# Statistics of x for the recurrent stage: made tile by tile in the experts' tail instead of at the stage's head

## The reference

```python
x = x + gate2[:, None, :] * grouped_moe(h, ...)      # end of the first block
...
def _rmsnorm(x, g):
    x32 = x.astype(jnp.float32)
    y = x32 * lax.rsqrt(jnp.mean(x32 * x32, axis=-1, keepdims=True) + EPS)
    return (y * g.astype(jnp.float32)).astype(x.dtype)

mem_n = _rmsnorm(mem, g_mem)
for _ in range(DEPTH):                               # DEPTH = 1
    h = _rmsnorm(x, g_mix)
    proj = h @ w_in
```

## Time and profile before

| | us |
|---|---|
| median of 3 runs | 2318.85 |
| lowest, highest | 2314.3, 2320.19 |
| the profiled execution | 2319.08 |
| its span | 2317.3 |
| PE, DVE, ACT, POOL busy | 2121.6, 1119.1, 864.4, 577.1 |

### The profile page before, as it was taken

One profiled execution on the slowest core, in us unless ns is written; L12 is line 12 of the kernel. 1 busy time (PEld: TensorE's weight loads), 2 busy tenths in 40 slices (PEclk: granted clock), 3 DMA queues, 4 the chain that ended last, 5 costly groups with the idle time before them and its releaser, 6 DMA issues. The chain is left out here.

```text
span 2317.3 us, 23519 instructions
## 1 busy us (share of the span) xinstructions
PE 2121.6 (92%) x9422; PEld 1601.8 (69%) x9422; DVE 1119.1 (48%) x1387; ACT 864.4 (37%) x1084; POOL 577.1 (25%) x195
## 2 busy tenths in 40 slices
PE   6997999999879999879999969899799998999997
PEld 3766755474358888767777747687388876887886
DVE  3344556646780234658888547405722245223223
ACT  4441223334222223457677437524423233221221
POOL 0421200130024344100000103430244343433431
PEclk9998999999989999889999989999799999999999
DMA  7223223231023233379999922231023232322210
GB/s 241 91 85 147 84 98 126 93 109 32 0 65 127 85 106 109 116 268 375 361 385 383 328 70 91 93 92 46 2 90 100 90 111 91 109 96 85 91 55 37
DMA packets 174702, 299.15 MB, mean 129 GB/s; under 512 B 8927, under 2 KB 66474, under 8 KB 174600
## 3 DMA queue, kind: packets, MB, share of 16 engines
q1 hardware_dynamic: 169256, 279.40, 35.4%
q0 software_dynamic: 3040, 9.93, 1.2%
q10 hardware_dynamic: 2304, 8.39, 0.9%
HBM read 274.57 MB, written 23.13 MB: 128 GB/s over the span
## 5 line engine op out<-in xcount | busy, mean ns | idle before, releaser
L130 POOL TENSOR_TENSOR region<-weights,region 128x2048 fp32r<-128x2048 f32 (+2 forms) x94 | 366.0, 3896 | 943.7 <-ACT region L124 764.5
L240 PE MATMUL ps<-region 128*128 128x512 f32 (+1 forms) x1336 | 530.8, 397 | 33.3 <-DVE region L130 10.9
L244 PE MATMUL ps<-region 128*128 128x512 f32 (+1 forms) x1336 | 520.6, 390 | 0.0
L243 PE MATMUL ps<-region 128*128 128x512 f32 (+1 forms) x1336 | 520.5, 390 | 0.0
L240 PEld LDWEIGHTS ps<-region 128*128 128x128 f32 x1336 | 259.6, 194 | 98.0 <-issue 19.4
L243 PEld LDWEIGHTS ps<-region 128*128 128x128 f32 x1336 | 259.5, 194 | 52.8 <-issue 4.1
L244 PEld LDWEIGHTS ps<-region 128*128 128x128 f32 x1336 | 259.2, 194 | 50.7
L124 ACT ACTIVATE region<-weights 128x2048 fp32r<-128x2048 f32 (+2 forms) x98 | 158.5, 1622 | 285.7 <-PE ps L244 236.8
L2870 DVE TENSOR_TENSOR region<-weights,region 128x2048 fp32r<-128x2048 f32 x92 | 209.4, 2289 | 71.2 <-ACT region L2794 71.1
L2794 ACT ACTIVATE region<-weights 128x2048 fp32r<-128x2048 f32 x92 | 176.2, 1917 | 89.4 <-PE ps L2711 30.8
L281 PE MATMUL ps<-region 128*128 128x512 f32 x480 | 190.1, 396 | 7.0 <-DVE region L3769 4.4
(11 more groups left out here) (417 smaller groups left out, 2773.0 us busy)
## 6 DMA issues: line engine op xcount, KB each, us to landing
weights<-w_in SPq DMA_DIRECT2D x54, 1024.0 KB, 5.2
weights<-moe_w_gate SPq DMA_DIRECT2D x32, 1024.0 KB, 7.6
weights<-moe_w_up SPq DMA_DIRECT2D x32, 1024.0 KB, 8.9
weights<-moe_w_down SPq DMA_DIRECT2D x32, 1024.0 KB, 7.0
weights<-w_mod SPq DMA_DIRECT2D x24, 1024.0 KB, 5.6
weights<-w_mlp_in SPq DMA_DIRECT2D x16, 1024.0 KB, 5.2
weights<-w_mlp_out SPq DMA_DIRECT2D x16, 1024.0 KB, 5.0
h_slots<-region SPq DMA_DIRECT2D x16, 512.0 KB
```

The source lines that it names most:

```text
L130: eng.tensor_tensor(flat(self.part(K, n, 1)), flat(self.ring.view(n)), flat(self.part(K, n, 0)).bitcast(F32), ALU.subtract).then_inc(self. ...
L240: ins = pe.matmul(out, l_hi, r_hi, start=(start and k == 0), stop=False)
L243: pe.matmul(out, l_hi, r_lo, start=False, stop=False)
L244: ins = pe.matmul(out, l_lo, r_hi, start=False, stop=(stop and k == kt - 1))
```

## The change

The sums are made for one tile of 128 tokens at a time in the tail of `moe_stage`. For each tile ACT squares all 1024 channels in one instruction (`square`), POOL folds the eight channel tiles to four and to two (two additions, 512 and 256 wide), PE sums the two over the channels with products by ones (`squares`), ACT takes the root (`root`) and DVE inverts it. PE turns tile 0 between `memory(1)` and `memory(2)`, DVE adds tile 0 to x before it combines tiles 2 and 3, and ACT takes its squares of tiles 0 and 1 before the copy of `memory(3)`, those of 2 and 3 behind it. In the overflow stage the statistics are made anew, with `NormStats`, after the loop and within the branch. `lru_stage` makes none: it scales two tiles at once and rounds its second weight chunk after four tiles of the norm.

```diff
@@ moe_stage @@
+    x_sq = (K.at(148, KD, P), K.at(164, KD, P))
+    def token_sums(t):
+        return K.ps[:, MEM_BANKS[t % 2], t * P:(t + 1) * P]
@@ POOL, behind the gathers @@
+            for t in range(ST):
+                sq = x_sq[t % 2]
+                pool.wait_ge(x_squared, t + 1)
+                pool.tensor_tensor(sq[:, 0:4, :], sq[:, 0:4, :], sq[:, 4:8, :], ALU.add).then_inc(x_folded, 1)
+                pool.wait_ge(x_folded, 2 * t + 1)
+                pool.tensor_tensor(sq[:, 0:2, :], sq[:, 0:2, :], sq[:, 2:4, :], ALU.add).then_inc(x_folded, 1)
@@ PE @@
-            memory(0, False)
-            memory(1, False)
-            arrived(K, pe, n_mem + 2)
-            memory(2, True)
-            for t in range(ST):
+            def turn_out(t):
                 pe.wait_ge(summed, t + 1)
                 if t >= 2:
                     pe.wait_ge(x_added, KD * (t - 1))
...
+            def squares(t):
+                pe.wait_ge(x_folded, 2 * t + 2)
+                if t >= 2:
+                    pe.wait_ge(x_rooted, t - 1)
+                for k in range(2):
+                    ins = pe.matmul(token_sums(t), K.ones[:, :], x_sq[t % 2][:, k, :], start=(k == 0), stop=(k == 1))
+                ins.then_inc(x_summed, 1)
+            memory(0, False)
+            memory(1, False)
+            turn_out(0)
+            arrived(K, pe, n_mem + 2)
+            memory(2, True)
+            turn_out(1)
+            turn_out(2)
+            turn_out(3)
             pe.wait_ge(y_out, 2 * NEXP)
             memory(3, False)
-            pe.wait_ge(mem_out, 1)
-            pe.matmul(K.ps[:, MEM_BANKS[0], 0:1], K.ones[:, :], K.ones[:, 0:1], start=True, stop=True).then_inc(r.used, 2)
+            pe.wait_ge(mem_out, 3)
+            pe.matmul(K.ps[:, MEM_BANKS[2], 0:1], K.ones[:, :], K.ones[:, 0:1], start=True, stop=True).then_inc(r.used, 2)
+            for t in range(ST):
+                squares(t)
@@ ACT @@
+            def square(t):
+                act.wait_ge(x_added, KD * (t + 1))
+                if t >= 2:
+                    act.wait_ge(x_summed, t - 1)
+                act.activation(x_sq[t % 2], K.xT[:, :, t * P:(t + 1) * P], ACT.Square).then_inc(x_squared, 1)
+            def root(t):
+                act.wait_ge(x_summed, t + 1)
+                act.activation(K.rstd[:, t * P:(t + 1) * P], token_sums(t), ACT.Sqrt, bias=K.eps, scale=1.0 / D)\
+                    .then_inc(x_rooted, 1)
             memory(2)
+            square(0)
+            square(1)
             memory(3)
+            root(0)
+            square(2)
+            root(1)
+            square(3)
+            root(2)
+            root(3)
@@ DVE @@
+            combine(0)
+            combine(1)
+            add_to_x(0)
+            combine(2)
+            combine(3)
+            for t in range(1, ST):
+                add_to_x(t)
+            for t in range(ST):
+                root = K.rstd[:, t * P:(t + 1) * P]
+                dve.wait_ge(x_rooted, t + 1)
+                dve.reciprocal(root, root).then_inc(x_inverted, 1)
+            dve.wait_ge(x_inverted, ST)
@@ moe_overflow_stage @@
+    stats = NormStats(K, stat_signals, K.xT, S, K.at(108, 2, S), K.rstd, 6)
...
         with eng.If(count > 0):
             with eng.Fori(0, count) as i:
                 body(i)
+            if again:
+                again(count)
@@ lru_stage, PE @@
-            for t in range(KD):
-                stats.add(pe, t)
@@ lru_stage, ACT @@
             split.high(K, act, n0)
-            for t in range(KD):
-                stats.square(act, t)
+            norm.act(act, 0, 4)
             split.high(K, act, n0 + 1)
-            stats.root(act)
-            norm.act(act)
+            norm.act(act, 4, KD)
@@ lru_stage, DVE @@
+            norm.scale(dve, 0)
+            norm.scale(dve, 1)
             split.low(K, dve, n0)
-            stats.invert(dve)
-            dve.wait_ge(stats.inverted, 1)
-            norm.dve(dve, 0, 4)
+            norm.rest(dve, 0)
+            norm.rest(dve, 1)
+            norm.dve(dve, 2, 4)
             split.low(K, dve, n0 + 1)
```

More of the change, by code:

```diff
@@ L24 @@
 NMARKS = 16
-NSIG = 24
+NSIG = 29
 VECS = [("c", 8), ("c_ctx", 8), ("b_mod", 48), ("norm1_g", 8), ("norm2_g", 8), ("q_norm_g", 1), ("k_norm_g", 1),
@@ L2644, in moe_stage @@
      y_out, even_y_stored, odd_y_stored, weighed, summed, x_turned, x_added, mem_done, mem_out, mem_rec, mem_root,
-     scaled) = K.signals(24)
+     scaled, x_squared, x_folded, x_summed, x_rooted,
+     x_inverted) = K.signals(29)
     rows_in, y_stored = (even_rows_in, odd_rows_in), (even_y_stored, odd_y_stored)
@@ L2911, in _, with combine @@
             low_hidden(NEXP - 1)
-            for t in range(ST):
+            def combine(t):
                 b = both[:, t, 0, :]
@@ L2916, in _, with add_to_x @@
                     .then_inc(summed, 1)
-            for t in range(ST):
+            def add_to_x(t):
                 dve.wait_ge(x_turned, t + 1)
@@ L2922, in _ @@
                                              mod_col(K, 5, c), x, ALU.mult, ALU.add).then_inc(x_added, 1)
-            dve.wait_ge(x_added, ST * KD)
+            combine(0)
[10 more added lines that the diff above has]
+            dve.wait_ge(x_inverted, ST)
 def moe_order():
@@ L2939, in moe_overflow_stage @@
     T = K.T
-    came, freed, gu_done, silu_done, up_done, hid_done, down_done, x_added = K.signals(8)
+    came, freed, gu_done, silu_done, up_done, hid_done, down_done, x_added, *stat_signals = K.signals(12)
     FT = 4
@@ L2945, in moe_overflow_stage, with experts @@
     LOADS = 7
+    stats = NormStats(K, stat_signals, K.xT, S, K.at(108, 2, S), K.rstd, 6)
     def part(s):
         return w[:, s, :].rearrange("p (t c) -> p t c", c=HALF)
-    def experts(eng, body):
+    def experts(eng, body, again=None):
         count = eng.value_load(K.over_list[0:1, NEXP:NEXP + 1], min_val=0, max_val=NEXP)
@@ L2989, in body, with again @@
                                 for k in range(FT)]).then_inc(down_done, 1)
-            experts(pe, body)
+            def again(count):
+                for t in range(KD):
+                    stats.add(pe, t)
+            experts(pe, body, again)
         @block.scalar
@@ L2998, in body, with again @@
                     act.activation(silu[:, f % 2, :], K.ps[:, f % 2, :], ACT.Silu).then_inc(silu_done, 1)
-            experts(act, body)
+            def again(count):
+                act.wait_ge(freed, count + 1)
+                for t in range(KD):
+                    stats.square(act, t)
+                stats.root(act)
+            experts(act, body, again)
         @block.vector
@@ L3023, in body, with again @@
                 dve.memset(prod[:, 0, 2:3], 0.0).then_inc(freed, 1)
-            experts(dve, body)
+            def again(count):
+                stats.invert(dve)
+                dve.wait_ge(stats.inverted, 1)
+            experts(dve, body, again)
 def lru_stage(K):
@@ L3034, in lru_stage @@
     n0, nq = r.first("lru"), r.first("qm")
-    stats = NormStats(K, norm_signals[0:4], K.xT, S, K.at(92, 4, S), K.rstd, 5)
-    norm = NormApply(K, norm_signals[4:7], K.xT, (K.h_hi, K.h_lo), gain_of(K, "g_mix_2"), None, K.rstd, K.at(100, KD, S))
+    norm = NormApply(K, norm_signals[0:3], K.xT, (K.h_hi, K.h_lo), gain_of(K, "g_mix_2"), None, K.rstd, K.at(100, KD, S))
     nX, nG = (n0, n0 + 2), (n0 + 4, n0 + 6)
```

## The result

The changed kernel takes 2304.84 us, the median of 6 runs (2298.67 to 2308.34); the kernel before 2316.75 (2313.39 to 2320.19, 6 runs). The ratio is 0.9945, 95% interval 0.993 to 0.996, a gain of 12.7 us (9.3 to 16.2).

What follows compares the result with a forecast made beforehand. TensorE, busy 92% of a 2317.3 us span, bounds the kernel, so changes pay where it stands still. Head -13.35 plus tail +5.5 gives -7.9 us, from 2319.08 to 2311.2, stated as 2311.0 for the median; range 2306 to 2316.

Steps and rivals of the forecast that it cites:

- Rival 1: Overflow stage: its instruction page was held up by weight transfers, some 1.5 us of queueing, so 2309.5 us; chance 0.17.
- The rule on fetches: Overflow stage: a taken branch to outside the two instruction pages held must wait for a fetch; no size given.
- The head: Start of the recurrent stage to its first product: 5.07 us instead of 18.42, saving 13.35.
- The tail: End of the experts' stage: the added statistics chain makes it end 5.5 us later.
- The order's 3.4 us: Experts' tail: with tile 0 turned and added earlier, the last product of the memory ends 3.4 us earlier.
- the chain behind the last product: Experts' tail: copy, table load, roots, squares, foldings, small products and reciprocal, from 1345.2 to 1355.7.
- Rivals 2 to 4: ACT stalls at table switch, 2312.4 us (0.07); slow clock lasts longer, 2313.5 (0.12); POOL foldings cost more, 2325.7 (0.06).

Runs made afterwards that it cites:

- e1: The kernel before with ten one-column TensorE products (40 instructions) added ahead of the overflow branch; ratio 0.9987.
- e3: The changed kernel with 24 one-column TensorE products (96 instructions) added inside the overflow branch that is not taken; ratio 0.9962.
- e4: The changed kernel with the product that frees two weight slots moved behind the four sums, so two transfers fall into the overflow stage; ratio 0.9961.
- e2: The kernel before with two weight chunks issued in the recurrent stage instead of at the end of the experts' tail; ratio 0.9989.
- e5: The changed kernel with the old order of the experts' tail: tile 0 turned after the third memory product, all tiles combined before additions; ratio 0.9952.
- e7: The changed kernel with all four squares and the table load ahead of ACT's copy of the last memory product; 2298.86 us, ratio 0.9909.

## Why the prediction was wrong

- **The step that failed** is "The overflow stage stays at 6.07 us (1350.16 to 1356.23): its new instructions stand inside the branch not taken." It fell to 2.22. The step took a body that is never run to cost nothing, and the jump over it at its old price. What counts is also how many TensorE instructions stand ahead of the branch and in it: in the profiles e1 makes the stage 3.85 us shorter with padding alone, and e3 makes it 3.17 longer again with padding that is never run. Each was done with one size of padding, so where the page's edges lie was not measured. The run times do not show this step by themselves (e1 has no gain inside its interval, e3 and e4 have the same ratio). Had I asked the view of the branch's line for its own duration, the 4.79 us would have been in the sum's bounds.
- **Rival 1** had the right place and the wrong cause and price. It gave 1.5 us to queueing behind the weights. Without transfers the jump still takes 3.71 us (e2) and 4.12 (e3) against 4.79, so queueing is 0.7 to 1.1 us and is not what went: with the weights back the stall stays away (e4). The prediction also had the landing early: the packet ran from 1353.34 to 1354.45 and so landed 4.3 us into the stage, not 3.4.
- **The rule on fetches** was cited with the row and then used for nothing but queueing. By the Trainium skill (Runtime: NRT & Kernel Launch, Instruction fetch mechanics) a taken branch stalls if its target lies outside the two pages held. The traces agree with it: the jump takes 0.46 to 0.48 us in the seven kernels in which no page's packet came during it, and 3.71 to 4.79 us in the three in which one did (before, e2, e3).
- **The head** was right: 4.98 us measured, 5.07 forecast, 13.44 saved against 13.35.
- **The tail** was right: +5.34 against +5.5. Its prices by what the trace has: table load 1.28 (1.28), root 0.37 (0.36), square 1.05 (1.05), foldings 1.27 and 0.72 (1.29 and 0.65), small products 1.22 (0.9; the granted clock stood at 0.50 there), reciprocal 0.95 (0.95). The order's 3.4 us is borne out by before and after (3.3 to 3.8) and by e5 (3.0 to 3.6, through a disturbed profile), and the chain behind the last product took 10.7 us against 10.5.
- **Rivals 2 to 4** fell. The gap between the load's end and the root is 0.01 us, and e7 recovers 1.22 us and not 2.7. The foldings took 2.0 us a pair, 4.0 for the four where 3.9 was priced. The low clock lasted shorter, not longer: in the 5.4 us behind the first product the mean clock is 0.70 and 17 records run, against 0.50 and 13 before.
- **Range and chances.** The only price given to a shorter stage was rival 1's 1.5 us, not the 3.84 that it fell by. The right sum with it, -11.9, is 2307 from the earlier runs of before (2318.85), just inside the range; what puts the time below it is the 2.1 us by which before itself came out lower in the paired runs. The gain was mis-sized by the stage, and that the time fell outside the range and not just inside it is chance.

## What to carry to other kernels

In this kernel a jump decided at run time had a price of its own on the engine with most instructions, and the trace shows it as the duration of that engine's compare-and-branch; read it before calling a stage fixed. An edit that adds instructions ahead of the jump or in its body turned that price on or off (here 3.6 to 4.3 us of jump, 3.2 to 3.9 of stage), so test an edit's gain with padding alone before crediting the edit. And look at what stands behind the last product of a stage: moving the squares and the table load ahead of it made the tail 5.6 to 5.8 us shorter here.

## What the runs showed of the hardware that I had not expected

TensorE's jump over the branch, a body of some 400 instructions (96 products of four records each), takes 0.46 to 0.48 us when no page is fetched in it, and 3.71 to 4.12 us when one is, with the DMA engines nearly idle. In e2 the page's packet (16 KB, 1.27 us) starts 1.05 us after the jump began, and the jump ends 1.39 us after the packet does; in before and e3 that last part is 1.39 and 1.41. Eight records of small products (L2796) took 1.14 us right behind the last product of the memory, at a granted clock of 1.00, and four took 1.22 us after 4.3 idle us, at 0.50.
